# Sample loop anew: shared difference tile for two sequences, transpositions through three PSUM banks

## What is computed

```python
# native sparse attention: 8 query heads in 2 groups, three branches, each with its own keys and values
o_cmp, p_cmp = compressed_attend(q_nsa, cmp_all, pos, cmp_pe, w_cmp1, w_cmp2)  # 32-token blocks -> gelu(blocks @ w1) @ w2
sel_idx = select_blocks(p_cmp, pos, sel_all.shape[1])                          # best 16 of 17 blocks
o_sel = selected_attend(q_rot, sel_all, sel_idx, pos)
o_win = local_attend(q_rot, win_all, pos, wpos)                                # last 512 tokens
o_nsa = g[..., 0:1] * o_cmp + g[..., 1:2] * o_sel + g[..., 2:3] * o_win
# differential attention: 4 heads, two softmax maps a head
s = einsum('bqhcd,bkhcd->bhcqk', q_diff, k_all) * SCALE
p = masked_softmax(s, kp <= qp)
o_diff = rmsnorm(einsum('bhqk,bkhe->bqhe', p[:, :, 0] - lam * p[:, :, 1], v_all), diff_subln)
x = x + (gate_nsa * (o_nsa @ w_br_nsa) + gate_diff * (o_diff @ w_br_diff)) @ w_out
```

## Time and profile before

| | us |
|---|---|
| median of 3 runs | 1476.13 |
| lowest and highest | 1474.38, 1478.85 |
| span of the profiled execution | 1471.4 |
| sample loop, hidden start of turn 0 to branch products | 251.96 to 464.63 |
| experts, from the first product | 546.6 on |
| PE, DVE, ACT, POOL busy over the span | 1398.4, 483.2, 285.1, 106.4 |

### The profile page before, as it was taken

One profiled execution on the slowest core, in us unless ns is written; L12 is line 12 of the kernel. 1 busy time (PEld: TensorE's weight loads), 2 busy tenths in 40 slices (PEclk: granted clock), 3 DMA queues, 4 the chain that ended last, 5 costly groups with the idle time before them and its releaser, 6 DMA issues.

```text
span 1471.4 us, 20712 instructions
## 1 busy us (share of the span) xinstructions
PE 1398.4 (95%) x7398; PEld 621.9 (42%) x7398; DVE 483.2 (33%) x1132; ACT 285.1 (19%) x600; POOL 106.4 (7%) x217
## 2 busy tenths in 40 slices
PE   7999999998898999999999999999999999999987
PEld 3446555676674453333333333333333333333322
DVE  1114475555543644221221331331222222213314
ACT  2003344435444030101100110010001011001002
POOL 1000122434300000000000000000000000000000
PEclk9999999999999999999999999999999999999999
DMA  7335676788887759999999999999999999999996
GB/s 265 114 114 180 232 169 222 218 252 252 274 265 252 277 230 427 427 429 428 429 428 428 428 428 428 429 428 429 428 428 428 428 430 428 428 429 428 428 428 256
DMA packets 92800, 509.60 MB, mean 346 GB/s; under 512 B 18986, under 2 KB 37906, under 8 KB 67506
## 3 DMA queue, kind: packets, MB, share of 16 engines
q1 hardware_dynamic: 77522, 481.12, 81.4%
q0 software_dynamic: 15232, 27.89, 5.9%
HBM read 502.38 MB, written 10.62 MB: 349 GB/s over the span
## 4 chain that ended last, share of the span: by engine, by line
PE 78%; DMA 15%; DVE 3%; issue 2%; ACT 2%; SPq 0%; DVEq 0%; ACTq 0%
PE PS L1398 24%; PE PS L1428 11%; DMA arena<-in_w_gate_up 9%; PE PS L1372 6%; PE PS L350 5%; DMA arena<-in_w_down 4%; PE PS L2092 4%; PE PS L596 4%; PE PS L1364 3%; PE PS L529 3%; PE PS L1260 2%; PE PS L1087 2%; PE PS L359 1%; PE PS L1415 1%; PE PS L2068 1%
## 5 line engine op out<-in xcount | busy, mean ns | idle before, releaser
L1398 PE MATMUL PS<-arena 128*64 128x512 f32 x2048 | 456.0, 595 | 13.9 <-DMA arena<-in_w_gate_up 12.9
L1398 PEld LDWEIGHTS PS<-arena 128*64 128x64 f32 x2048 | 141.7, 137 | 294.7 <-issue 263.2
L1428 PE MATMUL PS<-arena 128*64 128x512 f32 x1024 | 226.9, 594 | 2.3 <-DMA arena<-in_w_down 2.2
L1854 DVE TENSOR_SCALAR arena<-PS 128x512 f32<-128x512 f32 x32 | 22.1, 691 | 450.8 <-PE PS L1407 449.8
L1428 PEld LDWEIGHTS PS<-arena 128*64 128x64 f32 x1024 | 71.7, 137 | 150.5 <-issue 144.3
L529 PE MATMUL PS<-arena 128*128 128x128 f32 x496 | 71.6, 281 | 19.4 <-ACT arena L770 11.2
L1372 PE MATMUL PS<-arena 128*128 128x512 f32 (+1 forms) x180 | 84.2, 608 | 0.0
L1364 PE MATMUL PS<-arena 128*128 128x512 f32 (+1 forms) x192 | 79.4, 617 | 4.5 <-ACT arena L1564 3.7
L350 PE MATMUL PS<-arena 128*128 128x512 f32 (+1 forms) x192 | 79.5, 575 | 2.2 <-DMA arena<-in_w_in 2.2
L1221 POOL COPY arena<-arena 96x64 bf16 (+1 forms) x34 | 7.8, 233 | 987.1 <-PE PS L1435 943.1
L1775 DVE TENSOR_TENSOR arena<-PS,arena 128x512 f32<-128x512 f32 x32 | 21.8, 687 | 162.2 <-PE PS L1380 161.2
(11 more groups left out here) (292 smaller groups left out, 1294.2 us busy)
## 6 DMA issues: line engine op xcount, KB each, us to landing
arena<-in_w_gate_up SPq DMA_DIRECT2D x128, 2048.0 KB, 20.1
arena<-in_w_down SPq DMA_DIRECT2D x62, 2048.0 KB, 22.1
arena<-in_w_in SPq DMA_DIRECT2D x9, 2048.0 KB, 12.5
arena<-in_cache_diff_k SPq DMA_DIRECT2D x64, 256.0 KB, 5.5
arena<-in_cache_diff_v POOLq DMA_DIRECT2D x64, 256.0 KB, 5.6
arena<-in_cache_cmp_kv POOLq DMA_DIRECT2D x64, 128.0 KB, 4.0
arena<-in_cache_sel_kv SPq DMA_DIRECT2D x64, 128.0 KB, 3.0
arena<-in_state_win_kv SPq DMA_DIRECT2D x8, 512.0 KB, 5.8
```

The lines of the kernel that those rows point to most:

```text
L1398: last = nc.tensor.matmul(bank(2 + role + 2 * u)[64 * h:64 * h + 64], hTm[:, k, BS * u:BS * u + BS], gu_w[:, k, D * role + 512 * h:D * rol ...
L1428: last = nc.tensor.matmul(bank(6 + u)[64 * h:64 * h + 64], aT[u][:, c % 4, 64 * (c // 4):64 * (c // 4) + 64], down_w[u][c // 4][:, c % 4, ...
```

## The change

- The difference queries of the two sequences of a turn stand in one 32-column block a head (16 columns each, zero where the other's are), and `dif_scores(0)` and `dif_scores(1)` accumulate into the same scores. New keys stand ahead of the old ones in the tile. One mask, one maximum, one exp, 9 instead of 18 transpositions; the values are multiplied for each sequence, then scaled with a 0/1 mask, added, joined and normed once.
- Transposition groups have names, an engine each (`LOOP_ENGINE`) and rotate through banks 0, 1 and 7; a group waits for the one three before it. Two small product results and the join go through the same rotation.
- PE's order: both difference scores stand at the head of the turn, with sequence 1's keys transposed among the first hidden steps and all else that needs transposing among the second.
- DVE turns the key part of the next compressed pages in two halves early in the turn, and their value part near its end, behind the variance.
- POOL: queries right behind sequence 1's compressed pages, the values of both sequences, then the next compressed pages. SP: both sequences' keys ahead of selected and window pages.
- ACT visits Gelu twice in a turn.
- In the last turn gates are loaded ahead of `w_out`; the branch products use other banks.

The diff, cut; "..." stands for what is left out, removed lines of the loop (they are printed above) among it; blank lines and waits on an engine's own last instruction are left out too.

```diff
+    dif = np.full((128, NB // 2, NS), NEG)
+    for i in range(NB // 2):
+        dif[:, i] = np.where((kb[None] == 2 * i + (p[:, None] // 16) % 2) & (kt[None] <= t[:, None]), 0, NEG)
...
+        KEYW, WINW = NS + PAST, WIN + NS
+        e_key, e_win = ebuf[:, 0:KEYW], ebuf[:, KEYW:KEYW + WINW]
+        s_key, s_new, s_old = PS[:, 7 * 512 - KEYW:7 * 512], PS[:, 7 * 512 - KEYW:5 * 512], PS[:, 5 * 512:7 * 512]
+        s_win = PS[:, 3 * 512:3 * 512 + WINW]
+        hidden_at = (bank(2)[:, 0:4 * NCC], bank(3)[:, 0:4 * NCC])
+        s_cmp, grouped = bank(2)[:, 256:256 + NCC], bank(2)[:, 320:320 + NCC]
+        pv_nsa = bank(2)[:, 0:192].rearrange("p (b d) -> p b d", b=3)
+        pv_dif = (bank(2)[:, 192:320], bank(2)[:, 320:448])
+        ptl = ptb.rearrange("p (j r) -> p j r", r=128)
+        J_WIN, J_NEW, J_NEWD = 8, 12, 15
+        T_BANK = (0, 1, 7)
+        SCORES, EXPS, VALUES = 3, 4, 3
+        SC_D0, SC_D1, SC_NSA = 1, 2, 3
+        EXP_DIF, EXP_CMP, EXP_SEL, EXP_WIN = 1, 2, 3, 4
+        PV_D0, PV_D1, PV_NSA = 1, 2, 3
+        LOOP_GROUPS = ("kd0", "kd1", "kd2", "kd3", "kd4", "kd5", "kd6", "kd7", "kc", "sel0", "sel1", "sel2", "sel3", "win0", "pd0", "win1", "pd1", "pd2", "vc",
+                       "nk0", "nk1", "ps0", "ps1", "jo", "pw", "pm", "nk2", "nk3", "nk4", "nk5", "nk6", "nk7", "o")
+        LOOP_ENGINE = "ADADADAD" "A" "ADAD" "AADAAD" "ADADDAD" "AADAAAD"
+        L_TP = len(LOOP_GROUPS)
+        LAST_GROUPS = tuple(g for g in LOOP_GROUPS if g[:2] != "nk")
+        FIRST_KEYS = tuple(range(-NPAGE, 0))
...
+        def group_engine(n, final=False):
+            if n < 0:
+                return "AD".index(LOOP_ENGINE[L_TP + n])
+            return "AD".index(LOOP_ENGINE[LOOP_GROUPS.index(LAST_GROUPS[n]) if final else n])
...
                 dk_pages(i, 0)
+                dk_pages(i, 1)
                 sel_pages(i)
                 win_pages(i)
-                dk_pages(i, 1)
...
             values_in(0, 1, True)
             with pool.Fori(1, PAIRS_OF_SEQ - 1) as i:
                 cmp_pages(pool, i, 1)
+                queries_of(i)
                 values_in(i, 0)
-                queries_of(i)
+                values_in(i, 1)
                 cmp_pages(pool, i + 1, 0)
-                values_in(i, 1)
             cmp_pages(pool, PAIRS_OF_SEQ - 1, 1)
+            queries_of(PAIRS_OF_SEQ - 1)
             values_in(PAIRS_OF_SEQ - 1, 0)
-            queries_of(PAIRS_OF_SEQ - 1)
             values_in(PAIRS_OF_SEQ - 1, 1)
...
-            def tp(i, n, items, order=ident):
-                past(pe, l_out[n % 2], i * (L_TP // 2) + (8 + n) // 2)
+            def group_place(i, n, final=False):
+                e = group_engine(n - 3, final)
+                if not (isinstance(i, int) and i == 0 and n < 3 - NPAGE):
+                    past(pe, l_out[e], groups_out(e, i, n - 3, final))
+                return bank(T_BANK[(NPAGE + n) % 3])
+            def tp(i, name, items, final=False, n=None):
+                place = group_place(i, group_at(name, final) if n is None else n, final)
                 for src, col in items:
                     r, c = src.shape[0], src.free_size()
-                    last = nc.tensor.transpose(bank(n % 2)[0:c, col:col + r], src, order[0:r, 0:r])
+                    last = nc.tensor.transpose(place[0:c, col:col + r], src, ident[0:r, 0:r])
                 last.then_inc(l_tp, 1)
...
                 def dif_scores(b):
...
                     for k0 in (0, 512):
                         for h in range(4):
...
+                            last = nc.tensor.matmul(s_old[32 * h:32 * h + 32, k0:k0 + 512], cur_dif[:, b, 32 * h:32 * h + 32], kdT[:, h, k0:k0 + 512],
+                                                    start=(b == 0), stop=(b == 1))
+                    if b == 1:
+                        for b2 in range(2):
+                            for h in range(4):
+                                last = nc.tensor.matmul(s_new[32 * h:32 * h + 32], cur_dif[:, b2, 32 * h:32 * h + 32], kdnT[:, h, SEQ:NTOK],
+                                                        start=(b2 == 0), stop=(b2 == 1))
                     last.then_inc(l_sc, 1)
...
+                def compressed_scores():
+                    group_out(pe, i, "kc", final)
+                    for b in range(2):
+                        last = nc.tensor.matmul(s_cmp[64 * b:64 * b + 64], cur_raw[:, b, :], kcT[:, b, :], start=True, stop=True)
+                    last.then_inc(l_cmp, 1)
+                def group_sums():
+                    pe.wait_ge(l_pn, i + 1)
+                    nc.tensor.matmul(grouped, const("rsum"), pn, start=True, stop=True).then_inc(l_grp, 1)
                 pe.wait_ge(l_cur, (i + 1) * 3)
...
+                l_out_done(pe, i, -2)
+                past(pe, l_exp, i * EXPS)
                 dif_scores(0)
                 pe.wait_ge(cmp_turned, i * 16 + 16)
...
+                for l in range(CB // 2):
+                    hidden(0, l)
+                    if l % 2:
+                        group(f"kd{l // 2}")
+                l_out_done(pe, i, group_at("kd7", final), final)
+                dif_scores(1)
+                pe.wait_ge(l_gelu, i * 2 + 1)
+                place = group_place(i, group_at("kc", final), final)
                 for g in range(2):
...
+                    last = nc.tensor.matmul(place[64 * g:64 * g + 64, 0:2 * NCC], w2[:, 0, :], hid[:, 0, g, :], start=True, stop=True)
+                last.then_inc(l_tp, 1)
+                between = {0: "sel0", 2: "sel1", 4: "sel2", 6: "sel3", 8: "win0", 9: "pd0", 10: "win1", 11: "pd1", 12: "pd2"}
+                for l in range(CB // 2):
+                    hidden(1, l)
+                    if l in between:
+                        group(between[l])
+                    if l == 1:
+                        compressed_scores()
+                    if l == 7:
+                        group_sums()
+                l_out_done(pe, i, group_at("sel3", final), final)
+                past(pe, l_exp, i * EXPS + EXP_DIF)
...
+                l_out_done(pe, i, group_at("win1", final), final)
+                pe.wait_ge(l_gelu, i * 2 + 2)
                 for b in range(2):
                     nc.tensor.matmul(s_win[64 * b:64 * b + 64, 0:WIN], cur_rot[:, b, :], winT[:, b, :], start=True, stop=True)
                 for b in range(2):
                     last = nc.tensor.matmul(s_win[64 * b:64 * b + 64, WIN:WINW], cur_rot[:, b, :], kwT[:, SEQ:NTOK], start=True, stop=True)
                 last.then_inc(l_sc, 1)
...
+                l_out_done(pe, i, group_at("pd2", final), final)
+                pe.wait_ge(l_sum, i + 1)
+                dif_values(0)
+                place = group_place(i, group_at("vc", final), final)
+                for b in range(2):
+                    for g in range(2):
+                        last = nc.tensor.matmul(place[0:NCC, 128 * b + 64 * g:128 * b + 64 * g + 64],
+                                                hid[:, 1, g, NCC * b:NCC * b + NCC], w2[:, 1, :], start=True, stop=True)
+                last.then_inc(l_tp, 1)
                 dif_values(1)
...
+                group("nk0")
+                group("nk1")
+                group("ps0")
+                group("ps1")
+                pe.wait_ge(l_on, i + 1)
+                place = group_place(i, group_at("jo", final), final)
+                nc.tensor.matmul(place[:, 0:128], cmat, onrm, start=True, stop=True).then_inc(l_tp, 1)
+                group("pw")
+                group("pm")
+                for pg in range(2, 6):
+                    group(f"nk{pg}")
                 if final:
                     arrived(pe, "br")
                     branch_products(pe, 0, 0)
-                join(1)
-                next_keys(4, 5, 6, 7)
+                l_out_done(pe, i, group_at("pm", final), final)
+                nsa_values()
+                group("nk6")
+                group("nk7")
                 if final:
                     branch_products(pe, 0, 1).then_inc(br_full, 1)
-                pe.wait_ge(l_odn, i + 1)
-                tp(i, G_OD, [(odn[:, b, :], 128 * b) for b in range(2)])
+                group("o")
...
                 table(ACT.Gelu_apprx_tanh, 0)
...
+                ev("kd0", "kd2", "kd4", "kd6")
                 gelu(0)
-                ev(2)
+                table(ACT.Exp, 1)
+                ev("kc", "sel0")
+                exp(3, EXP_DIF, e_key, s_key, lsum[:, 3:4])
+                exp(1, EXP_CMP, pn, s_cmp, lsum[:, 1:2])
+                ev("sel2", "win0", "pd0", "pd1", "pd2")
+                table(ACT.Gelu_apprx_tanh, 0)
                 gelu(1)
-                ev(4, 6)
                 table(ACT.Exp, 1)
...
+                exp(2, EXP_SEL, e_key, s_key, lsum[:, 2:3])
+                exp(0, EXP_WIN, e_win, s_win, lsum[:, 0:1])
+                ev("nk0", "ps0", "pw")
+                group_out(act, i, "jo", final)
+                st(nc.scalar.activation(sqj, osq, ACT.Square, accum_out=lsum[:, 5:6]), l_sq)
```

(42 more changed lines are left out.)

478 lines of the change are left out of this document (186 added, 292 removed).

## The result

The changed kernel takes 1521.88 us (median of 4 runs, 1518.91 to 1527.24) against 1475.93 for the kernel before beside it: ratio 1.0315, 95% interval 1.0289 to 1.0341. It is slower, as forecast, but by 46 us and not by 22. The profiled execution has a span of 1518.1 us, 3.8 under the median, where 1493.7 was forecast.

What follows compares the result with a forecast made beforehand. Sample-loop time passes undiminished to the kernel, with PE busiest in a turn and POOL's queue to watch. Turns +16.6, last turn +0.3, start 0, clock +5.4: +22.3, span 1493.7; plus 4.7 to the median, 1498.4 us, range 1481 to 1514.

Steps and rivals of the forecast that it cites:

- the late turning of the value half: DVE turns it at 39.7 of the turn, before at 18.6; next hidden start 16.6 later, so a turn is 54.6.
- the edge: Turn boundary: PE idles for queries behind POOL's copies, then for pages DVE turns; turn 54.6 against 53.06.
- the group sums: Second place, in hidden 1 of turns 1 and 2: PE's sums wait behind DVE's late pages, 6.0 in each.
- The free turn: PE's turn if nothing is late: 46.3 against 53.06.
- The branch weights' wait: Last turn: weights issued 9.5 later, behind hidden 1; PE waits 6 to 9; turn 53.8 against 53.5, +0.3.
- the landing of 4.0 us: Compressed pages from issue to landing: the earlier rows' median of 4.0, used at the edge and the second place.
- Rival (c): DMA contention on top, with loads in flight together at the edge: five waits with 3 us more, 1513; chance 0.13.
- SP, turn 0: sum 0 with bounds -2 and +3: SP's moved queue: 2 us allowed for sequence 1's keys in turn 0, against 2.6 gained with three banks.
- The clock: 1.8 each for three waits: PE's lower clock after long idle: behind two waits in hidden 1 and the branch weights' wait, 5.4 in all.
- (a): Rival: only the turn edge waits, sequence 0's pages come in time; 1482.8; chance 0.12.
- (b): Rival: pages are never late and the banks' gain comes through, three turns of 46.3; 1460; chance 0.05.
- (d): Rival: the merge does nothing measurable, PE work falls 1.4 a turn at most; 1470 without new wait; chance 0.04.

Runs made afterwards that it cites:

- the experiment with the selected pages: Changed kernel, but SP issues a turn's 16 selected pages only when all compressed pages of that turn have landed: 1515.89 us, ratio 1.0254.
- The fillers of the right size: Changed kernel with dummy matmuls at turn edges, seven behind the output transposition and four behind the first difference scores: 1518.2 us, ratio 1.0292.
- POOL's mended order: Changed kernel, but POOL issues the next pair's first compressed pages between the two sequences' values instead of behind both: 1502.56 us, ratio 1.018.
- the kernel with both steps mended: Changed kernel with the value half turned right behind hidden 1 and POOL's order of the kernel before: 1478.31 us, ratio 1.0015.

## Why the prediction was right in sign and half in size

**Right.** That the experts' stream passes the loss on undiminished. That the late turning of the value half is the cause: undone alone it gives back 38 us, made alone in the kernel before it costs 41. That there are two places, the edge (turns 0 to 2) and the group sums (turns 1 and 2), and which engines release PE there. The issue times: 10.4 counted and 10.6 found to the eighth page, and from there to the fourth page of the next pair 25.9 (2.3 + 15 x 1.23 + 1.2 + 4.0) against 25.3. The free turn: 46.3 counted, 46.9 to 47.2 found. The branch weights' wait: 6 to 9 forecast, 8.4 found, and the 8 us that PE wins there are lost as said. Two readings in the forecast are inexact, and nothing hangs on them: the first slice at 427 in the earlier trace rows is number 15, counted from 0, not 14; and the 18.6 us of the kernel before are counted from the hidden start, the 39.7 from the first score, so that the value half was moved by 19.4 and not by 21.1.

**Wrong in size.** Along the chain that set the time, in the order of the sum:

| stretch | counted | found | what was longer |
|---|---|---|---|
| hidden start to value half, turn 0 | 38.0 | 44.0 | keys' wait 4.4, low clock after it 1.6 |
| value half to value half, turn 0 to 1 | 60.6 | 68.8 | landing 10.1 for 4.0 (5.7 net of quicker issues), low clock 2.5 |
| the same, turn 1 to 2 | 60.6 | 66.1 | landing 9.0 for 4.0 (4.1 net of quicker issues), low clock 1.4 |
| value half to last hidden start | 16.6 | 18.8 | landing 6.9 for 4.0 (2.2 net of quicker issues) |
| last turn | 53.8 | 59.3 | weights issued 2.9 late by the low clock at the edge, landed 0.5 later, first product 5.26 for 3.44 |
| branch products to the end | 1006.8 | 1009.5 | open |

The excesses add up to 30.1, with 0.3 that the start was earlier to take off; of them the forecast had 5.4 in its clock term. That leaves 24.4, the difference between 1493.7 and 1518.1.

The step that failed is **the landing of 4.0 us**, the median of the earlier trace rows. It measured 10.1 and 9.0 at the second place and 6.9 at the last edge, and that makes 12.0 of the 24.4 (5.7, 4.1 and 2.2 in the table). That median came from a kernel in which the three pages' groups were spread over the turn; the change bunches keys, selected, value and compressed pages, and the long landings of turn 1 fell to 4.3 and 3.6 when the neighbour in the DMA engines was held back. Rival (c) names this mechanism and gave it 0.13 and 3 us at each of five waits. Its chance should have been the forecast's: the DMA share of 0.82 in a turn was at hand, and in the kernel before it is 1.04 from 314 to 324 with pages and keys in flight together. The place was wrong too, since at the edges of turns 1 and 2 a longer landing costs nothing, as the experiment with the selected pages shows. It costs at the second place.

**SP, turn 0: sum 0 with bounds -2 and +3** was the second. The keys of sequence 1 were 4.4 late and the products behind that wait ran at the lower clock, 1.6 more: 6.0, twice the upper bound.

**The clock: 1.8 each for three waits.** At the three counted places the price was near. From start to start, and against the same instructions at the full clock, PE loses 3.0 and 1.9 behind the two waits for the group sums and 1.7 on the first branch product: 6.6 where 5.4 was counted. What failed are places set at 0. One is the keys' wait. The other is the edge: the forecast let its slow stretch fall on the first scores, which have time to spare, but PE idles again behind these, and the hidden products of the next turn run at the lower level as well, 3.1, 1.8 and 2.9 lost at the three edges. In turns 1 and 2 the wait before the group sums takes that up. In the last turn nothing does: hidden 1 ends 2.9 later, and the branch weights are issued later by as much. The fillers of the right size show both.

The Trainium skill (TensorE: Matmul & The Clock Gate, Why this matters for your kernels) has idle gaps bring the slow rate back, and I had set an early stretch of the earlier trace rows, where 14 us with 5 of work kept the clock, against it. In the trace after, each of the waits of 3.9 us or more in the loop is followed by matmuls at the lower level (2.05 or 1.89 for four hidden products, where 1.02 is usual), and those of 1.2 are not. Behind the one of 2.4 the first four products still take 1.39, and the next four 1.89. Here the rule holds.

**The rivals.** (a) would be a kernel with the edge's waits only; that is what POOL's mended order gives, and it takes 1502.6, not 1482.8, its turn 0 being 5.9 longer for the keys. (b), no page late, is the kernel with both steps mended: 1478, not 1460. Its turns of 51 are 4 longer than the free turn, with window pages waited for and a DMA share of 0.89 and 0.90. The loads of a turn come to 46 us of all DMA engines' time in these 51.6, so a turn of 46.3 would leave hardly any room beside them. That this is its bound is argued, not shown. (d), that merge and banks bring next to nothing, is true of the banks, 2.4 us; the merge wasn't tried apart from them.
